# Three openings of a two-block transformer kernel: two output tiles taken slice by slice together, and the low parts moved in VectorE's order

## The chip, the cores and the metric

The kernel runs on one core of one Trainium2 chip. The metric is the device time of one execution in microseconds (us), the median of several runs. The core has five engines that work side by side and meet through semaphores: TensorE (PE, matmuls; PEld is its weight load), VectorE (DVE), ScalarE (ACT), GpSimd (POOL) and SyncE (SP), which here issues most of the DMAs.

## What is computed

The reference runs two transformer blocks on 1024 tokens of width 1024, all in float32. The first block matters here:

```python
h = rmsnorm(x, mix_norm_g)
q, k, v, g, u = split(h @ w_in)                      # 4 heads of retention, 4 pooling groups
y_ret  = silu(g) * head_rmsnorm(retention(rope(q), rope(k), v), ret_gn_g)
y_pool = pool_mixer(u, pool_w, pool_scale)           # means over 2, 4, 8, 16 tokens, then 128x128 products
x = x + concat(y_ret, y_pool) @ w_out                # "the output projection"
x = x + cross_attn(rmsnorm(x, xa_norm_g), mem_n, ...)
x = x + conv_glu_ffn(rmsnorm(x, ffn_norm_g), ...)    # "the feed-forward"
```

The second block (a gated delta rule layer and an attention layer with forget gates) follows and isn't touched.

## The kernel before

Activations lie feature-major: 8 slices (KT = 8) of 128 features by 1024 tokens. Every projection is cut into output tiles of 128 features, and a tile is 48 matmuls of 512 columns: 8 slices, 2 halves of the tokens, and 3 products each (`dot3`, L517 to L519), since each float32 operand is split into a high part (rounded to the matmul's fp32r form) and a low part (the rest), and high by high, high by low and low by high are added. The activation's parts are `h_hi` (made by ACT) and `h_lo` (made by DVE from `h_hi`); a weight tile is loaded by SP into one of two buffers `w_raw`, and POOL makes `w_hi` (L450) and `w_lo` (L452) of it (`split_slot`). Tile t uses weight buffer and PSUM accumulator t % 2. So the weights of tile t+2 can be split only once PE is through with tile t (`pe_slot`), and its matmuls can begin only once tile t was copied out of PSUM (`tile_out`, `tile_added`) and the split is done (`w_split`).

The order on each engine is written out by hand. PE counts the 16 groups of a tile with `s` (`among`) and does the small matmuls of other stages between them.

Launch. SP loads weight tile 0, the 8 slices of x, then weight tile 1, in this order. POOL's queue issues the vectors, the positions and then four sets of constants (L444), before it splits weight tile 0. ACT makes `h_hi` slice by slice (L1249) and then squares x (L1204). DVE computes the rotation angles of the sine (L1823 to L1842), then the 8 low parts (L1846), the sum of the squares (L1777, L1780), the reciprocal root of the first norm (L1851), the angles of the cosine (L1828 to L1840), multiplies both tables, once ACT has taken their sine, by the norm (L1858), and rotates q (L1866 to L1875) and k (L1866 to L1869). PE takes tile 0 slice by slice as the low parts come (`fresh`), then tile 1; the norm's sums (`token_sums`, L591) stand at s = 28, near the end of tile 1, and the norm is spread over the partitions (`spread`, L597) after it. The norm doesn't scale h; it is applied to what comes out of the tiles. Tiles 2 and 3 follow, then the first head's work, which begins with transposes of the rotated k (`turn8`, L617).

Output projection. DVE's last pooling step (`pool(3)`) comes before the low parts of its input (L1960). PE takes tile 20, the first of the projection, over slices 0 to 6, multiplies the last pooling group by its weights (`pool_product(3)`, L662, at s = 13), and waits for slice 7, which comes of that product through ACT and DVE. After the last low part ACT loads the memory tokens `memx` and x again (L1336, L1338), ACT squares and DVE sums `memx`, and DVE adds tile 20 to the loaded x (L1968); tile 22 waits for that addition, tile 23 for that of tile 21.

Feed-forward. After the last addition (L2016) DVE adds the square of the slice before, makes the 8 low parts (L2022) and adds the last square. PE takes tiles 0 and 1 (of the feed-forward), then the norm's sums and its spread; ACT copies the norm out (L1426), DVE copies tile 0 out with it (L2049), and tile 2 waits for that.

## Time and profile before

| | us |
|---|---|
| median of 3 runs (lowest, highest) | 3104.93 (3104.66, 3107.49) |
| the profiled execution | 3107.14 |
| its span, first to last instruction | 3105.3 |
| PE busy in it | 2891.3 (93%) |
| DVE / POOL / ACT busy | 1534.7 / 1057.7 / 802.7 |
| mean granted clock of PE | 0.967 of full |

PE is busy nearly all the time, so what counts is where it stands still or runs at half its clock; the three stages of the change lie at 0 to 90, 319 to 385 and 773 to 820 us of the span.

### The profile page before, as it was taken

The numbers are of one execution on the slowest core, as the hardware profiler recorded it, in microseconds if no ns is written. First come the engines' busy times: TensorE is split into PE (matmuls) and PEld (weight loads), VectorE is DVE, ScalarE is ACT, GpSimd is POOL, SyncE is SP. The second block draws the span as 40 slices with busy tenths as digits, with TensorE's granted clock in tenths as the row PEclk, the third lists the DMA queues.
The fourth block names the chain that finished last, engine by engine and source line by source line (L and its number), as shares of the span: only waits on it lengthen the run. The fifth ranks groups of instructions, "written<-read, shape, count | busy, mean of one in ns | idle before, by whom it ended". The sixth has DMA issues, their size and how long they took to land.

```text
span 3105.3 us, 35553 instructions
## 1 busy us (share of the span) xinstructions
PE 2891.3 (93%) x14278; PEld 2340.3 (75%) x14278; DVE 1534.7 (49%) x1903; ACT 802.7 (26%) x1137; POOL 1057.7 (34%) x473
## 2 busy tenths in 40 slices
PE   7999888989999999999988999999986999999996
PEld 5887677767788888888767888888774777777774
DVE  7334514122666665566845555666537344444434
ACT  4231202231100000000343434444322333333331
POOL 4232366214344444444411212222235333333223
PEclk9999999999999999999989999999997999999997
DMA  3111222001111111111212112222121111011112
GB/s 128 35 35 34 108 75 74 29 14 48 41 48 44 46 47 47 47 47 47 95 56 59 61 52 68 64 64 65 51 90 74 35 35 35 35 40 43 34 35 109
DMA packets 94228, 170.26 MB, mean 55 GB/s; under 512 B 30192, under 2 KB 56976, under 8 KB 93968
## 3 DMA queue, kind: packets, MB, share of 16 engines
q1 hardware_dynamic: 85120, 135.81, 13.4%
q10 hardware_dynamic: 8464, 30.48, 2.5%
q8 instruction: 100, 1.64, 0.2%
q0 software_dynamic: 512, 2.07, 0.2%
q14 instruction: 32, 0.26, 0.0%
HBM read 149.39 MB, written 18.94 MB: 54 GB/s over the span
## 4 chain that ended last, share of the span: by engine, by line
PE 80%; DVE 11%; POOL 3%; issue 3%; ACT 3%; DMA 1%; POOLq 0%; ACTq 0%; DVEq 0%; SPq 0%
PE gemm L517 18%; PE gemm L518 17%; PE gemm L519 17%; PE small L518 3%; PE small L517 3%; PE small L519 3%; PE small L591 3%; PE small L1095 2%; PE small L1117 2%; PE small L967 1%; DVE norm L1780 1%; PE small L1105 1%; POOL xres L495 1%; PE small L617 1%; DVE xres L2530 1%
## 5 line engine op out<-in xcount | busy, mean ns | idle before, releaser
L517 PE MATMUL gemm<-h_hi,w_hi 128*128 128x512 f32 x2688 | 1142.2, 425 | 89.1 <-DVE h_lo L1790 43.4
L518 PE MATMUL gemm<-h_lo,w_hi 128*128 128x512 f32 x2688 | 1074.7, 400 | 0.0
L519 PE MATMUL gemm<-h_hi,w_lo 128*128 128x512 f32 x2688 | 1073.8, 399 | 0.0
L450 POOL TENSOR_TENSOR w_hi<-w_raw,unit_col 128x1024 fp32r<-128x1024 f32 x174 | 341.3, 1962 | 1602.3 <-PE gemm L519 1452.0
L517 PEld LDWEIGHTS gemm<-h_hi,w_hi 128*128 128x128 f32 x2688 | 515.7, 192 | 210.1 <-issue 64.9
L519 PEld LDWEIGHTS gemm<-h_hi,w_lo 128*128 128x128 f32 x2688 | 512.8, 191 | 123.5
L518 PEld LDWEIGHTS gemm<-h_lo,w_hi 128*128 128x128 f32 x2688 | 515.5, 192 | 105.2 <-issue 6.5
L452 POOL TENSOR_TENSOR w_lo<-w_raw,w_hi 128x1024 fp32r<-128x1024 f32 x174 | 466.8, 2683 | 13.7
L486 POOL TENSOR_TENSOR w_hi<-w_raw,unit_col 128x1024 fp32r<-128x1024 f32 x32 | 60.6, 1893 | 374.6 <-PE gemm L519 374.6
L2049 DVE TENSOR_TENSOR norm<-gemm,norm 128x1024 f32<-128x1024 f32 x44 | 53.9, 1226 | 192.1 <-PE gemm L519 189.8
L517 PE MATMUL small<-act_hi,w_hi 128*128 128x512 f32 x352 | 139.3, 396 | 0.0
L518 PE MATMUL small<-act_lo,w_hi 128*128 128x512 f32 x352 | 139.3, 396 | 0.0
L519 PE MATMUL small<-act_hi,w_lo 128*128 128x512 f32 x352 | 139.3, 396 | 0.0
L2080 DVE TENSOR_TENSOR xres<-small,xres 128x1024 f32<-128x1024 f32 x88 | 107.5, 1222 | 58.1 <-PE small L519 58.0
L2058 DVE SCALAR_TENSOR_TENSOR head<-norm,vec,head 128x1024 f32<-128x1024 f32 x44 | 124.6, 2832 | 3.9 <-DVE head L2054 1.2
L1432 ACT ACTIVATE head<-head 128x1024 f32<-128x1024 f32 x22 | 23.3, 1061 | 374.0 <-DVE head L2062 374.0
L2516 DVE SCALAR_TENSOR_TENSOR xres<-small,rstd_cols,xres 128x128 f32<-128x128 f32 x64 | 22.5, 351 | 192.6 <-PE small L1095 172.9
L591 PEld LDWEIGHTS small<-const,norm 128*128 128x128 f32 x688 | 91.9, 211 | 30.7 <-DVE norm L1780 17.3
L591 PE MATMUL small<-const,norm 128*128 128x1 f32 x688 | 89.2, 260 | 25.9 <-DVE norm L1780 18.9
L1662 ACT ACTIVATE xres<-xres,stat 128x128 f32<-128x128 f32 (+3 forms) x64 | 49.7, 777 | 227.0 <-DVE stat L2522 226.1
L1437 ACT ACTIVATE act_hi<-head 128x1024 fp32r<-128x1024 f32 x22 | 23.4, 1062 | 265.5 <-DVE head L2067 265.5
L1117 PEld LDWEIGHTS small<-xres 128*128 128x128 f32 x576 | 74.1, 191 | 8.4 <-ACT xres L1735 2.8
(379 smaller groups left out, 3758.3 us busy)
## 6 DMA issues: line engine op xcount, KB each, us to landing
w_raw<-w_stream SPq DMA_DIRECT2D x206, 512.0 KB, 3.2
x_spill<-xres ACTq DMA_DIRECT2D x16, 512.0 KB, 2.6
xres<-x_spill ACTq DMA_DIRECT2D x16, 512.0 KB, 7.6
xres<-x_t SPq DMA_DIRECT2D x8, 512.0 KB, 13.0
xres<-x_t ACTq DMA_DIRECT2D x8, 512.0 KB, 10.1
xres<-g_rows SPq DMA_DIRECT2D x8, 512.0 KB, 3.8
norm<-g_rows SPq DMA_DIRECT2D x8, 512.0 KB, 3.7
mt_plane<-xres SPq DMA_DIRECT2D x8, 512.0 KB, 3.2
```

What stands on the lines that cost most here:

```text
L450: nc.gpsimd.tensor_tensor(whi[s][:, :, :], raw[s][:, :, :], unit, ALU.mult).then_inc(w_hi_done, 1)
L452: nc.gpsimd.tensor_tensor(wlo[s][:, :, :], raw[s][:, :, :], whi[s][:, :, :].bitcast(F32), ALU.subtract).then_inc(w_split, 1)
L486: nc.gpsimd.tensor_tensor(whi[s][:, :, :], raw[s][:, :, :], unit, ALU.mult).then_inc(w_hi_done, 1)
L517: mm(dst, w_hi, a_hi, start=first, stop=False)
L518: mm(dst, w_hi, a_lo, start=False, stop=False)
L519: return mm(dst, w_lo, a_hi, start=False, stop=last)
L591: last = mm(dst[:, n:n + 1], ck(src, n), ones[:, 0:1], start=True, stop=True)
L1095: last = mm(pa[:, c:c + w], ck(yt[:, g, :], q), H[:, g % 2, c:c + w], start=True, stop=True)
L1117: last = mm(ck(pb, 4 + q % 4), ck(X4(0), b), ck(X4(5), b), start=(b == 0), stop=(b == q))
L2049: V.tensor_tensor(a[:, 2:2 + S], gp[v][:, :], WIDE_FF, ALU.mult).then_inc(tile_out, 1)
L2058: V.scalar_tensor_tensor(c, a[:, 1:1 + S], at("ff_w", 2 * PAIRS + q), c, ALU.mult, ALU.add).then_inc(ff_taps, 1)
L2080: V.tensor_tensor(xres[:, m, :], ps[m % 2][:, :], xres[:, m, :], ALU.add).then_inc(down_ev, 1)
```

## The change

`gemm_pair` takes two tiles together: for each slice first tile t, then tile t+1, so a slice carries 12 matmuls, not 6. Three places use it: tiles 0 and 1 of the launch, tiles 20 and 21 of the output projection, tiles 0 and 1 of the feed-forward. The rest moves with it: the norm's sums and spread of the launch from s = 28 and 31 to 36 and 39 (in tile 2), on PE and on ACT, those of the feed-forward to s = 25 and 28 of the pair's 32 groups, the last pooling product to s = 19 (after slice 4 of the pair). On DVE the low parts and the sums of squares of the launch go ahead of all angles; the low parts 0 to 3 of the output projection go into `pool(3)`, behind its copy out of PSUM and ahead of the pooling itself; one addition of squares in the feed-forward goes from ahead of the low parts to between the last two. On POOL's queue the four loads of constants go between the splits of weight tiles 0 and 1. SP's order stays. ACT waits for the sums of squares before it copies out tile 0 of the launch.

```diff
@@ POOL
-            for dst, src in ((const[:, :], consts), (row[:, :], rows.broadcast_to([P, N_SMALL])),
-                             (small_raw[:, :, :], small_w), (poolw[:, :, :], pool_w)):
-                pool.dma_start(dst, src).then_inc(const_loaded, 16)
...
-            for s in range(2):
-                split_slot(s, s, 1)
+            split_slot(0, 0, 1)
+            for dst, src in ((const[:, :], consts), (row[:, :], rows.broadcast_to([P, N_SMALL])),
+                             (small_raw[:, :, :], small_w), (poolw[:, :, :], pool_w)):
+                pool.dma_start(dst, src).then_inc(const_loaded, 16)
+            split_slot(1, 1, 1)
@@ PE
+            def gemm_pair(t, a_hi, a_lo, fresh, among=None):
+
+                for k in range(KT):
+                    pe.wait_ge(h_lo_done, KT * fresh + k + 1)
+                    for b in range(2):
+                        if k == 0:
+                            pe.wait_ge(w_split, t + b + 1)
+                        for c in range(2):
+                            at = slice(c * HALF, (c + 1) * HALF)
+                            last = dot3(gp[b][:, at], whi[b][:, k, :], wlo[b][:, k, :], a_hi[:, k, at], a_lo[:, k, at],
+                                        k == 0, k == KT - 1)
+                            if k == KT - 1 and c:
+                                last.then_inc(pe_slot, 1)
+                            if among is not None:
+                                among(4 * k + 2 * b + c)
...
-                    if w == 0 and s == 28:
+                    if w == 0 and s == 36:
                         pe.wait_ge(const_loaded, 64)
                         pe.wait_ge(sq_added, KT * (NMIX + 1))
                         token_sums(pa[:, 0:NB], N[:, 2, :]).then_inc(norm_mm, 1)
-                    if w == 0 and s == 31:
+                    if w == 0 and s == 39:
                         pe.wait_ge(norm_rstd, S_MIX + 1)
                         spread(pa, R_H).then_inc(norm_wide, 1)
...
-                for j in range(4):
+                if w == 0:
+                    gemm_pair(T_RET, hhi, hlo, HMIX, among)
+                for j in range(0 if w else 2, 4):
...
-                if s == 2 * (KT - 1) - 1:
+                if s == 19:
                     pool_product(3)
...
+                if i == 0:
+                    gemm_pair(T_WOUT, hhi, hlo, HRET, pool_last)
+                elif i == 1:
+                    continue
...
-            for q in range(4):
-                if q >= 2:
-                    pe.wait_ge(tile_out, EV_FF + q - 1)
-                gemm_tile(T_FF + q, q % 2, hhi, hlo, S, HFF if q == 0 else None)
-                if q == 1:
+            def ff_start(s):
+
+                if s == 25:
                     pe.wait_ge(sq_added, KT * (NFF + 1))
                     token_sums(pa[:, 0:NB], N[:, 2, :]).then_inc(norm_mm, 1)
+                if s == 28:
                     pe.wait_ge(norm_rstd, S_FF + 1)
                     spread(pa, R_H).then_inc(norm_wide, 1)
+
+            gemm_pair(T_FF, hhi, hlo, HFF, ff_start)
+            for q in range(2, 4):
+                pe.wait_ge(tile_out, EV_FF + q - 1)
+                gemm_tile(T_FF + q, q % 2, hhi, hlo, S)
@@ ACT
             act.wait_ge(h_lo_done, KT * (HMIX + 1))
+            act.wait_ge(sq_added, KT * (NMIX + 1))
@@ DVE
+            for k in range(KT):
+                dve.wait_ge(h_hi_done, KT * HMIX + k + 1)
+                V.scalar_tensor_tensor(hlo[:, k, :], xres[:, k, :], vc("mix_g", k), hhi[:, k, :].bitcast(F32), ALU.mult,
+                                       ALU.subtract).then_inc(h_lo_done, 1)
+            for k in range(KT):
+                add_square(NMIX, k)
             dve.wait_ge(pos_loaded, 16)
...
                     done(V.tensor_scalar(dst, dst, -math.pi, None, ALU.max))
-                    for k in range(KT):
-                        dve.wait_ge(h_hi_done, KT * HMIX + k + 1)
-                        V.scalar_tensor_tensor(hlo[:, k, :], xres[:, k, :], vc("mix_g", k), hhi[:, k, :].bitcast(F32), ALU.mult,
-                                               ALU.subtract).then_inc(h_lo_done, 1)
-                    for k in range(KT):
-                        add_square(NMIX, k)
                     dve.wait_ge(norm_root, NMIX + 1)
                     V.reciprocal(R_H, R_H).then_inc(norm_rstd, 1)
...
                 V.tensor_tensor(POOL_U[:, PAD:], gp[t % 2][:, :], WIDE_MIX, ALU.mult).then_inc(tile_out, 1)
+                if j == 3:
+                    for k in range(4):
+                        lo_part(HRET, k, yt[:, k, :], hhi, hlo)
...
-            for k in range(KT):
+            for k in range(4, KT):
                 lo_part(HRET, k, yt[:, k, :], hhi, hlo)
...
-                if m:
+                if 0 < m < KT - 1:
                     add_square(NFF, m - 1)
...
             for k in range(KT):
+                if k == KT - 1:
+                    add_square(NFF, KT - 2)
                 dve.wait_ge(h_hi_done, KT * HFF + k + 1)
```

## Rows read from the trace of the kernel before

**Rows 1.** Page, the chain that ended last, share of the span by engine.

```profile
PE 80%; DVE 11%; POOL 3%; issue 3%; ACT 3%; DMA 1%; POOLq 0%; ACTq 0%; DVEq 0%; SPq 0%
```

**Rows 2.** Waits of PE, 0 to 100 us: who, for whom, us, times, longest.

```profile
PE gemm L517 <- DVE h_lo L1846: 19.7, 1, 19.7
PE small L591 <- DVE norm L1780: 2.9, 1, 2.9
PE small L617 <- DVE head L1869: 2.5, 1, 2.5
```

**Rows 3.** Waits of PE, 280 to 358 us.

```profile
PE gemm L517 <- DVE h_lo L1790: 11.5, 2, 7.9
```

**Rows 4.** Waits of PE, 770 to 812 us.

```profile
PE gemm L517 <- DVE h_lo L2022: 6.5, 1, 6.5
PE gemm L517 <- DVE norm L2049: 2.4, 1, 2.4
```

**Rows 5.** Stretches: us, busy (count) of PE, PEld, DVE, ACT, POOL; clock, DMA, GB/s.

```profile
10.00:15.00 5.00, 0.00 (x0) 0.00 (x0) 4.63 (x6) 2.11 (x2) 0.00 (x0) 1.00 1.01 406
27.10:42.55 15.45, 15.45 (x68) 12.34 (x66) 14.93 (x9) 5.08 (x5) 10.22 (x6) 1.00 0.20 68
49.03:52.95 3.92, 3.92 (x10) 3.01 (x11) 3.34 (x5) 0.27 (x1) 0.00 (x0) 0.51 0.00 0
326.83:339.39 12.56, 12.56 (x43) 10.00 (x43) 6.66 (x6) 0.00 (x0) 0.00 (x0) 0.76 0.00 1
```

**Rows 6.** Timeline of POOL: start, us, instruction, [idle before <-releaser].

```profile
22.22 2.68 POOL L450 TENSOR_TENSOR w_hi<-w_raw,unit_col 128x1024 fp32r<-128x1024 f32 x1 [13.09 <-DMA w_raw<-w_stream]
24.98 3.26 POOL L452 TENSOR_TENSOR w_lo<-w_raw,w_hi 128x1024 fp32r<-128x1024 f32 x1
...
100.50 1.89 POOL L450 TENSOR_TENSOR w_hi<-w_raw,unit_col 128x1024 fp32r<-128x1024 f32 x1 [18.84 <-PE gemm L519]
102.48 2.38 POOL L452 TENSOR_TENSOR w_lo<-w_raw,w_hi 128x1024 fp32r<-128x1024 f32 x1
```

**Rows 7.** Timeline of DVE, launch.

```profile
11.71 0.69 DVE L1828 TENSOR_SCALAR yt<-yt 128x1024 f32<-128x1024 f32 x1
...
18.28 13.56 DVE L1846 SCALAR_TENSOR_TENSOR h_lo<-xres,vec,h_hi 128x1024 fp32r<-128x1024 f32 x8
...
32.95 12.72 DVE L1780 TENSOR_TENSOR norm<-norm 128x1024 f32<-128x1024 f32 x7
49.51 0.20 DVE L1851 RECIPROCAL rstd_cols<-rstd_cols 128x8 f32<-128x8 f32 x1 [3.83 <-ACT rstd_cols L1291]
...
63.22 2.36 DVE L1858 TENSOR_TENSOR yt<-yt,norm 128x1024 f32<-128x1024 f32 x2 [3.32 <-ACT yt L1300]
...
76.57 2.87 DVE L1869 TENSOR_TENSOR head<-head,xres 128x1024 f32<-128x1024 f32 x1
```

**Rows 8.** Timeline of ACT, launch.

```profile
44.01 1.00 ACT L1267 ACTIVATE yt<-gemm 128x1024 f32<-128x1024 f32 x1
```

**Rows 9.** Timeline of DVE, opening of the output projection.

```profile
325.46 8.03 DVE L1790 TENSOR_TENSOR h_lo<-yt,h_hi 128x1024 fp32r<-128x1024 f32 x7
...
354.81 1.22 DVE L1968 TENSOR_TENSOR xres<-gemm,xres 128x1024 f32<-128x1024 f32 x1
```

**Rows 10.** Timeline of ACT, opening of the output projection.

```profile
341.31 1.11 ACT L1282 ACTIVATE yt<-small,vec 128x1024 f32<-128x1024 f32 x1 [15.62 <-PE small L662]
...
349.60 0.73 ACT L1204 ACTIVATE head<-memx 128x256 f32<-128x256 f32 x2 [6.09 <-DMA memx<-mem_t]
```

**Rows 11.** Timeline of DVE, opening of the feed-forward.

```profile
776.17 11.75 DVE L2022 SCALAR_TENSOR_TENSOR h_lo<-xres,vec,h_hi 128x1024 fp32r<-128x1024 f32 x8
...
808.49 1.22 DVE L2049 TENSOR_TENSOR norm<-gemm,norm 128x1024 f32<-128x1024 f32 x1 [2.29 <-ACT norm L1426]
```

**Rows 12.** Timeline of PE, opening of the feed-forward.

```profile
803.81 1.84 PE L591 MATMUL small<-const,norm 128*128 128x1 f32 x16
806.24 1.09 PE L597 MATMUL small<-const,rstd_cols 128*128 128x128 f32 x8 [0.59 <-DVE rstd_cols L2026]
```

More of the change, by code:

```diff
@@ L686, in _ @@
                 among = ret_among(w)
-                for j in range(4):
+                if w == 0:
+                    gemm_pair(T_RET, hhi, hlo, HMIX, among)
+                for j in range(0 if w else 2, 4):
                     t = T_RET + 4 * w + j
-                    if t >= 2:
-                        pe.wait_ge(tile_out, t - 1)
-                    gemm_tile(t, t % 2, hhi, hlo, S, HMIX if t == 0 else None, among, 16 * j)
+                    pe.wait_ge(tile_out, t - 1)
+                    gemm_tile(t, t % 2, hhi, hlo, S, None, among, 16 * j)
             def pool_last(s):
-                if s == 2 * (KT - 1) - 1:
+                if s == 19:
                     pool_product(3)
@@ L709, in _ @@
                         pe.wait_ge(tile_out, EV_MEM + m_out + 1)
-                if kind == "x":
-                    gemm_tile(t, t % 2, hhi, hlo, S, HRET if i == 0 else None, pool_last if i == 0 else None)
+                if i == 0:
+                    gemm_pair(T_WOUT, hhi, hlo, HRET, pool_last)
+                elif i == 1:
+                    continue
+                elif kind == "x":
+                    gemm_tile(t, t % 2, hhi, hlo, S)
                 else:
@@ L1288, in _ @@
                         ret_tile(h, s // 16 - 1)
-                    if w == 0 and s == 28:
+                    if w == 0 and s == 36:
                         act.wait_ge(norm_mm, NMIX + 1)
                         A(R_H, pa[:, 0:NB], ACT.Sqrt, bias=eps[:, 0:1], scale=1.0 / D).then_inc(norm_root, 1)
-                    if w == 0 and s == 31:
+                    if w == 0 and s == 39:
                         act.wait_ge(norm_wide, W_MIX + 1)
```

## The prediction

> **What bounds the kernel now.** I read the page's chain first: PE carries 80% of it and DVE 11% [rows 1], so a change of order gains only where PE stands still, and loses wherever it makes PE stand. Next come PE's own waits in the three stages. At launch there are three: 19.7 us until the first low part, 2.9 us ahead of the norm's sums, 2.5 us ahead of the transposes of the rotated k [rows 2]. At the output projection PE waits twice for a low part, 7.9 and 3.6 us [rows 3]; at the feed-forward 6.5 us for the first low part and 2.4 us for the copy out of tile 0 [rows 4]. Third, PE's pace in stretches [rows 5]: 15.45 us hold 66 matmuls at full clock, 0.234 us each, so a tile of 48 is 11.2 us and a pair's slice of 12 is 2.8; with the clock granted at 0.51 (1.2 GHz of 2.4) nine take 3.92 us, 0.43 each. A matmul at the lower level costs 0.19 us more. Last, the timelines of POOL, DVE and ACT show what ends each wait.
>
> The views also show what no wait shows: the second weight tile is there late. POOL idles 13.09 us for its load, begins its split at 22.22 and ends it at 28.24 [rows 6]. Before the change that costs nothing, since tile 0 alone keeps PE busy from 19.7 on.
>
> **Launch, PE.** The low parts now follow `h_hi` as x arrives; the first is ready near 11 us, not 19.7, and the last near 23.5, not 31.84 (18.28 + 13.56 [rows 7]). But `gemm_pair` needs both weight tiles in slice 0. Six matmuls run, and then PE stands until the second split. SP's order is the same, and the loads run at 406 GB/s with the DMA engines full [rows 5], so the load ends at 22.2 as before; the constants, issued after split 0, still pass in its shadow. Split 2 meets a busy DVE as before (6.0 us [rows 6]); PE resumes at 27.9. Of the remaining 90 matmuls those of about 6 us run at the low level: in the stretch from 326.83, 42 matmuls take 12.56 us, which solves to 6.1 us at 0.427 [rows 5]. I take 14 x 0.427 + 76 x 0.2335 = 23.7, and tile 1 ends at 51.6, tile 0 at 50.2. Before, tile 1 ended at 53.0, with the 2.9 us wait and 9 slow matmuls in it [rows 2, 5]: 1.4 us gained.
>
> It is given back at once. The weights of tile 2 can be split only when tile 0 is through, now 1.4 us ahead of tile 1 and no longer a whole tile ahead. A split without a rival on DVE is 1.89 + 2.38 + 0.1 = 4.35 us [rows 6]; tile 2 starts at 50.2 + 4.4 = 54.6 (before 53.7), after a pause of 3 us. A pause of 2.87 us was followed by matmuls at the low level [rows 2, 5], so I let 4 us of tile 2 run there: 9 matmuls more dear by 0.19, 1.8 us.
>
> **Launch, the norm and the angles.** This is the term that decides. The sums stood at s = 28 and gave the reciprocal at 49.51 to 49.71 [rows 7]. At s = 36 they follow 15 matmuls of tile 2: 54.6 + 15 x 0.2335 + 1.8 = 59.9, plus the sums, 1.84 less overlap, 1.75 [rows 12], and ACT's root and the reciprocal, 0.5: 62.2. ACT is free by then: its six copies of tiles 0 and 1, 1.02 each [rows 8], start at 50.2 and end at 56.4. On DVE the cosine's seven steps stand behind that reciprocal. They took from 49.71 to 59.90 (63.22 less 3.32 idle), with a split beside them; the sine's same seven took 11.71 to 18.28, 6.6 us, without one [rows 7]. After: 62.2 + 6.6 = 68.8, with no split beside them, since tile 3's is over near 59. Three sines on ACT: 3.3, the 3.32 us for which DVE idled [rows 7]. From 72.1 DVE needs two table products and seven rotation steps: before, 63.22 to 79.44, 16.2 us, of which about 5.4 is blocking by splits, seen in one 1.23 us step that took 2.87 [rows 7] and two like it. So 10.8 bare. Tile 2 ends at 54.6 + 11.2 + 1.8 + 1.75 + 0.95 = 70.3 (spread 0.95 from [rows 12]), and its end starts a split that lies on the tables; tile 3 ends at 81.6, and its end starts another. I take 4.4 of blocking: 72.1 + 10.8 + 4.4 = 87.3. Before: 79.5 [rows 7]. PE, whose own path arrives at 82.3, turns k 7.8 us later than now. It then stood 5 us, not 2.5, and I add 0.7 for the clock: **launch +8.5 us**, between +2.8 (PE's own path, 82.3) and +11 (sums and 15 matmuls wholly at the low level).
>
> What PE's earlier start frees is thus hidden behind DVE's angles, which gain a place later in line: the low parts and squares end some 9 us earlier, but DVE then idles from about 45 to 62 for the root.
>
> By the Trainium skill (SBUF — State Buffer, Who interferes with whom), a VectorE instruction with two SBUF inputs and a GpSimd one that reads SBUF block each other wholly, whichever issues second. The trace agrees in kind: L1869 took 2.87 us beside a split [rows 7] and `w_lo` 3.26 beside busy VectorE against 2.38 [rows 6]. Taken to the letter, each step met would lose a whole 2.4 us, the two splits 4.8, and the launch would come to +8.9.
>
> **Output projection.** Low parts 0 to 3 move ahead of the pooling step: four of 1.15 us (8.03 / 7 [rows 9]), behind a copy out at 320.2. With the split of tile 21 on them, the first is ready at 322, not 326.7, and pooling ends at 330.3, not 325.5. PE starts 4.8 us earlier, at the low clock for some 5 us, and does slices 0 to 4 of the pair, 60 matmuls: 322 + 14.0 + 2.2 = 338.2; the product stood at 339.4, after 42 matmuls [rows 5]. It takes 1.9 us; ACT's scaling (1.11 [rows 10]) and high part and DVE's low part follow, 3.5 us, so the last low part is there at 343.6, 1.1 earlier. The pair is done at 348.7, where tile 21 was done at 357.6: nearly 9 us. But tile 22 waits for tile 20's addition to the reloaded x. The reload begins behind the last low part, its first tensor lands 4.8 us later (ACT idles 6.09 for it [rows 10]), then come eight squares and sums, and the addition stood at 354.81 to 356.03 [rows 9]. Less 1.1 and with up to 2 us of blocking by the split of tile 23, which now lies here, tile 22 starts between 354.9 and 357, I take 355.8: 1.8 gained of 8.9. And PE has stood 7 us, so 8 to 14 matmuls at 0.19 extra follow, 1.5 to 2.7 us. **Output projection +0.3**, from -1.5 to +2.
>
> **Feed-forward.** With one addition of squares (1.88 us beside a split) gone from ahead of it, low part 0 is ready at 776.4, where the first stood behind a 776.17 start and came at 779.6 [rows 4, 11]: 3.2 us. The second weight tile is split by 778.5, just in time for slice 0. 96 matmuls 22.4 + about 2.1 for the low clock + sums and spread 2.8 [rows 12], now inside the pair: end at 803.8, tile 0 at 802.4. Its split (4.4 to 5.3) lets tile 2 start at 807.4, where it started at 809.77, 2.4 us after the wait of [rows 4]. The addition of squares between low parts 6 and 7 costs 1.2 us that PE, at 2.8 us a slice, doesn't see. **-2.3 us**, from -4.6 (a clock that stays up) to -1.
>
> By the Trainium skill (TensorE: Matmul & The Clock Gate, HAM oscillation), waits that recur between bursts of matmuls send the gate back to half rate, and the ramp is paid each time. The trace agrees at [rows 5], clock 0.51 after a 2.87 us pause; by that rule all three pairs are followed by such a ramp, which is what the sums have, and each that failed to come would take 1.8 us off.
>
> **Sum.** +8.5 + 0.3 - 2.3 = +6.5 us. Everything after 820 us hangs on PE's chain and moves along. The profiled run took 3107.14 (span 3105.3 + 1.84), 2.2 over the median of 3104.93. Against its own time: 3113.6; for the median: 3104.93 + 6.5 = **3111.4**.
>
> **Rivals.** *The launch delay is half as long.* If the norm's sums come at 59 and the splits miss the rotation, k is ready at 83 to 84 and the launch costs 4; total +1 to +3, 3107. For it: the count of slow matmuls after a pause varies, 9 here and 14 there. Against: the seven cosine steps and the rotation are fixed, 17.4 us.
> *The clock stays up (the other side).* The pairs' pauses are near 3 us, and PE's 2.5 us wait at launch [rows 2] is the shortest known. If PE keeps 2.4 GHz through pauses of 3.2 us, decided at the end of tile 1, the launch costs 2.8 to 4.5, the output projection gains 1.5 to 2 by an earlier product, the feed-forward gains 2.1 in the pair and 1.9 after it, 6.3: total -3.5 to -9, middle 3099 to 3101. Against it stands the 2.87 us pause with its clock of 0.51.
> *It doesn't do what it says.* If the moved constants let the second weight tile come earlier, by at most 1.33 MB / 406 GB/s = 3.3 us (962 + 256 + 96 + 12 KB by their shapes), the launch moves by that: total +3.2, 3108. That needs them to pass after it; they are issued near 9 us, it lands at 22.
>
> **How the numbers follow.** Forecast 0.60, own range 3106 to 3116 (launch +4 to +11 with the other terms' middles, rounded in): slower by over 6.2 us 0.46 of it, the rest within. Half delay 0.18 and earlier weights 0.05, all within 0.2%. Clock stays up 0.17: 0.11 faster, 0.06 within. So slower 0.46, same 0.43, faster 0.11; 0.2% or 6.2 us is about what a measurement of this kernel can tell from none. The range takes in half of the other side's case: 3101 to 3117.
>
> **What would show it.** Launch: six matmuls near 11 us, PE idle until 28, tile 2 near 54.6 behind POOL's `w_lo`, the reciprocal of L1851's twin near 62, PE's wait for the rotated k at 5 us, ending near 87. If it ends at 80, the main term is wrong. Output projection: PE starts at 322, ends the pair near 349 and waits some 7 us for the addition; a wait for `w_lo` in its place would mean that the reload isn't the limit and gain 3 us more. Feed-forward: the wait for the first low part at 3.3 us in place of 6.5, and a wait for `w_lo` of 3.5 in place of 2.4 for the copy (all later positions shifted by the launch's term). The prediction fails if the cosine's steps aren't what PE waits for, or if the clock ignores the pauses.

## The result and the profile after

The changed kernel is slower: 3119.89 us median (3116.96 to 3121.6, 6 runs) against 3104.8 (3101.59 to 3111.26, 6 runs), a ratio of 1.0039 with the 95% interval 1.0029 to 1.0049, that is +12 us (9 to 15). The two medians lie 15.1 us apart; I go by the ratio, which has an interval, here and in all experiments. I had forecast 3111.4, +6.5. The direction was right and the size about half of what came. The median of the runs lies 2.9 us above the upper end of my range (3101 to 3117); the ratio applied to the median I started from gives 3117.0, its very edge.

The profiled run of the changed kernel has the lowest of its six times, 3116.96 us, and that of the kernel before one of the higher (3107.49; the table and the prediction have 3107.14, which no run took), so the two traces, 9.8 us apart in span, show less than the 12. The page of the changed kernel (first its span, then the chain by engine) looks like that of before [rows 1], and PE is busy for 2887.4 us against 2891.3; the sums don't tell the two apart:

```profile
span 3115.1 us, 35554 instructions
...
PE 80%; DVE 10%; POOL 3%; issue 3%; ACT 3%; DMA 2%; SPq 0%; POOLq 0%; ACTq 0%; DVEq 0%
```

PE's waits in the changed kernel, 0 to 100 us (who, for whom, us, times, longest), where [rows 2] stood:

```profile
PE gemm L517 <- POOL w_lo L449: 17.4, 2, 14.1
PE gemm L517 <- DVE h_lo L1849: 10.7, 1, 10.7
PE small L633 <- DVE head L1894: 7.0, 1, 7.0
```

280 to 370 us, where [rows 3] stood:

```profile
PE gemm L517 <- DVE xres L1996: 11.2, 1, 11.2
...
PE gemm L517 <- issue: 3.2, 1, 3.2
```

770 to 830 us, where [rows 4] stood ("issue" is here the first matmul of the pair, which starts as soon as the first low part is there):

```profile
PE gemm L517 <- POOL w_lo L449: 3.6, 1, 3.6
PE gemm L517 <- issue: 3.2, 1, 3.2
```

Launch: the 19.7 us until the first low part became 10.7, but 17.4 us for the weight splits came in, 14.1 in slice 0 for the second tile's and 3.3 behind the pair for the third's; the wait for the rotated k grew from 2.5 to 7.0. Output projection: one wait of 11.2 us for the addition of tile 20, which the kernel before didn't have. Feed-forward: 6.5 became 3.2, and the split, 3.6, took the place of the 2.4 for the copy.

The weights of each tile are split once on POOL. The start of the same split in both traces gives the time by stage:

| Where (split of the tile) | before | after | shift | of the stage |
|---|---|---|---|---|
| tile 20, end of the retention heads | 306.2 | 313.2 | +7.0 | launch +7.0 |
| tile 24, the third split after the pair | 369.1 | 379.5 | +10.4 | output projection +3.4 |
| tile 46 | 523.8 | 537.2 | +13.4 | memory tiles, first query tile +3.0 |
| feed-forward tile 4 | 823.3 | 833.2 | +9.9 | feed-forward -3.5 |
| end of span | 3105.3 | 3115.1 | +9.8 | rest -0.1 |

**Launch.** POOL's timeline (start, us, instruction, idle before): the load of the second weight tile ends at 22.0 and its split at 27.7, as before [rows 6]; the split for tile 2 can start only at 49.70, where before it started at 34.0, and PE takes tile 2 up at 54.2.

```profile
22.02 2.90 POOL L447 TENSOR_TENSOR w_hi<-w_raw,unit_col 128x1024 fp32r<-128x1024 f32 x1 [10.94 <-DMA w_raw<-w_stream]
24.99 2.67 POOL L449 TENSOR_TENSOR w_lo<-w_raw,w_hi 128x1024 fp32r<-128x1024 f32 x1
...
49.70 1.90 POOL L447 TENSOR_TENSOR w_hi<-w_raw,unit_col 128x1024 fp32r<-128x1024 f32 x1 [17.84 <-PE gemm L519]
51.67 2.34 POOL L449 TENSOR_TENSOR w_lo<-w_raw,w_hi 128x1024 fp32r<-128x1024 f32 x1
```

DVE: the reciprocal of the root, the table products after ScalarE's sines, the last step of the rotation of k, which came at 49.51, 63.22 and 76.57 [rows 7]:

```profile
59.92 0.20 DVE L1876 RECIPROCAL rstd_cols<-rstd_cols 128x8 f32<-128x8 f32 x1 [14.89 <-ACT rstd_cols L1316]
...
69.97 4.75 DVE L1883 TENSOR_TENSOR yt<-yt,norm 128x1024 f32<-128x1024 f32 x2 [3.32 <-ACT yt L1325]
...
85.81 1.23 DVE L1894 TENSOR_TENSOR head<-head,xres 128x1024 f32<-128x1024 f32 x1
```

ACT in the same stretch, the wide copy of the norm and the first sine:

```profile
62.68 1.03 ACT L1319 ACTIVATE norm<-small 128x1024 f32<-128x1024 f32 x1 [2.80 <-PE small L613]
...
66.68 1.06 ACT L1323 ACTIVATE yt<-yt 64x1024 f32<-64x1024 f32 x1 [1.67 <-DVE yt L1871]
```

The reciprocal is 10.4 us late, k 7.6. PE turns k at 87.18, where it was 79.58; its own path had arrived at 80.1.

**Output projection.** POOL's splits of tiles 22 and 23, then DVE from the first sum of the memory tokens to the two additions to x, where [rows 9] has the addition at 354.81:

```profile
353.68 1.90 POOL L447 TENSOR_TENSOR w_hi<-w_raw,unit_col 128x1024 fp32r<-128x1024 f32 x1 [22.48 <-PE gemm L519]
355.65 2.34 POOL L449 TENSOR_TENSOR w_lo<-w_raw,w_hi 128x1024 fp32r<-128x1024 f32 x1
357.95 2.08 POOL L447 TENSOR_TENSOR w_hi<-w_raw,unit_col 128x1024 fp32r<-128x1024 f32 x1
360.11 2.40 POOL L449 TENSOR_TENSOR w_lo<-w_raw,w_hi 128x1024 fp32r<-128x1024 f32 x1
```

```profile
355.39 0.34 DVE L1802 COPY head<-head 128x256 f32<-128x256 f32 x1 [5.37 <-ACT head L1228]
355.83 9.07 DVE L1805 TENSOR_TENSOR head<-head 128x256 f32<-128x256 f32 x7
364.82 2.35 DVE L1996 TENSOR_TENSOR xres<-gemm,xres 128x1024 f32<-128x1024 f32 x2
```

Seven sums took 9.07 us. In the kernel before the same seven took 3.60 (351.29 to 354.89). An unhindered one takes 0.42; of the seven here three took 2.45, 1.93 and 2.38, each beside one of POOL's last three instructions.

**Clock.** Stretches of the changed kernel (us; busy and count of PE, PEld, DVE, ACT, POOL; granted clock; DMA share and GB/s): the 15 matmuls of tile 2 of the launch that stand ahead of the norm's sums, tile 22, and the first query tile, then that query tile in the kernel before.

```profile
54.16:57.74 3.58, 3.58 (x16) 2.89 (x16) 0.00 (x0) 2.95 (x3) 3.50 (x2) 1.00 0.44 146
366.09:379.13 13.04, 13.04 (x48) 10.45 (x49) 1.08 (x1) 0.00 (x0) 0.00 (x0) 0.85 0.07 29
521.16:534.52 13.36, 13.36 (x48) 10.65 (x48) 7.12 (x3) 0.00 (x0) 5.96 (x2) 0.78 0.24 78
```

```profile
510.43:521.16 10.73, 10.73 (x48) 8.71 (x48) 7.16 (x3) 0.00 (x0) 6.00 (x2) 1.00 0.28 98
```

Tile 2 of the launch ran at full clock behind a pause of 3.2 us. Tile 22 follows a pause of 11.2 us and has a clock of 0.85, nine slow matmuls. The query tile's code isn't part of the change: 13.36 us in one trace at a clock of 0.78 and 10.73 in the other at 1.00, 2.6 us.

### The profile page after: what moved, and what is told of

The parts are those of the page before. It is cut to its first block, busy times and chain, and to the rows that moved or that the text cites. A ratio compares the mean times of both kernels' runs of the same rounds, so it can differ in the third digit from the quotient of the medians.

```text
span 3115.1 us, 35554 instructions
## 1 busy us (share of the span) xinstructions
PE 2887.4 (93%) x14278; PEld 2333.4 (75%) x14278; DVE 1537.7 (49%) x1903; ACT 803.2 (26%) x1137; POOL 1059.0 (34%) x473
## 4 chain that ended last, share of the span: by engine, by line
PE 80%; DVE 10%; POOL 3%; issue 3%; ACT 3%; DMA 2%; SPq 0%; POOLq 0%; ACTq 0%; DVEq 0%
PE gemm L517 18%; PE gemm L518 17%; PE gemm L519 17%; PE small L517 3%; PE small L518 3%; PE small L519 3%; PE small L607 3%; PE small L1119 2%; PE small L1141 2%; PE small L991 1%; PE small L1129 1%; POOL xres L495 1%; PE small L633 1%; DVE xres L2560 1%; DVE norm L1805 1%
```

## The experiments

Two theories stood at the start. A: the three parts of the change add up, the launch loses by the late norm, the output projection by blocked sums, the feed-forward gains. B: one of them is harmless, or its gain or loss is the clock's. Ratios below are to the kernel before, with 95% intervals; 0.001 is 3.1 us.

**1. The launch's part alone**, the kernel before with the POOL, ACT and DVE steps of the launch and tiles 0 and 1 as a pair.

```diff
-            for s in range(2):
-                split_slot(s, s, 1)
+            split_slot(0, 0, 1)
...
+            split_slot(1, 1, 1)
...
-                    if w == 0 and s == 28:
+                    if w == 0 and s == 36:
...
+                if w == 0:
+                    gemm_pair(T_RET, hhi, hlo, HMIX, among)
```

> The launch's part of the change alone (constants after split 0, tiles 0 and 1 as a pair, low parts and squares ahead of the angles, the norm's sums at s = 36). Theory A, the three parts add up: the wait for the rotated k ends near 87 us where it ended at 79.6 before, and every later stage is 7.0 us late; +7 us in the profile, ratio near 1.0023. Rival B, the launch is harmless and the loss of some 12 us comes from the other two parts: k ready by 80 us, ratio within 1.000 +- 0.001.

Measured: 1.0049 (1.0032 to 1.0066), 3121.63 us. A's direction stands; its size, 1.0023, lies below the interval. The trace shows why. The stretch that ran at full clock in the changed kernel (3.58 us for 15 matmuls) is here:

```profile
54.71:61.02 6.31, 6.31 (x16) 4.95 (x17) 0.00 (x0) 2.95 (x3) 4.08 (x2) 0.52 0.42 127
```

6.31 us at half clock, for the same code behind the same pause of 3.24 us. DVE's reciprocal and the last step of k:

```profile
63.19 0.20 DVE L1869 RECIPROCAL rstd_cols<-rstd_cols 128x8 f32<-128x8 f32 x1 [18.31 <-ACT rstd_cols L1309]
...
89.08 1.22 DVE L1887 TENSOR_TENSOR head<-head,xres 128x1024 f32<-128x1024 f32 x1
```

The reciprocal moves with it, to 63.19, and k is ready at 90.3: the launch costs 11.3 us in this trace (split of tile 20 at 317.5) and 7.0 in that of the changed kernel. In both, k comes 26.9 us after the reciprocal's end. Run 7, whose launch is that of the changed kernel, has the clock at 0.53 there too and costs 11.4. I had written 4 us of half clock into tile 2; what came was none, some (5.1 us for the 15 matmuls, in run 4), or all.

**2. The output projection's part alone.**

```diff
+                if i == 0:
+                    gemm_pair(T_WOUT, hhi, hlo, HRET, pool_last)
...
+                if j == 3:
+                    for k in range(4):
+                        lo_part(HRET, k, yt[:, k, :], hhi, hlo)
...
-            for k in range(KT):
+            for k in range(4, KT):
```

> The output projection's part alone (tiles 20 and 21 as a pair, low parts 0 to 3 inside the last pooling step, product at s = 19). Theory A, the split of tile 23's weights now lies on VectorE's eight sums of the memory tokens and blocks them: tile 20's addition ends 10 us after the reload's first tensor lands instead of 5, tile 22 starts 1.5 us later than in the kernel before (357.6), 8 to 14 slow matmuls follow: +3 to +4 us, ratio 1.0011. Rival B, as my forecast had it, the addition waits for the reload and its few sums alone: tile 22 starts 1 to 2 us earlier, total within +-1 us.

Measured: 1.0008 (0.9997 to 1.0019). PE's wait in its trace, 280 to 372 us:

```profile
PE gemm L517 <- DVE xres L1991: 11.2, 1, 11.2
```

Tile 22 starts at 359.0 and not at 357.6, nine slow matmuls follow, and the third split after the pair is 3.5 us late: A, and not my forecast. The interval alone, +2.5 us (-1 to +6), wouldn't have told.

**3. The feed-forward's part alone.**

```diff
+            gemm_pair(T_FF, hhi, hlo, HFF, ff_start)
+            for q in range(2, 4):
...
-                if m:
+                if 0 < m < KT - 1:
...
+                if k == KT - 1:
+                    add_square(NFF, KT - 2)
```

> The feed-forward's part alone (its tiles 0 and 1 as a pair, the norm's sums and spread inside it, one addition of squares moved). Theory A: the wait for the first low part falls from 6.5 to 3.2 us, a wait of 3.6 us for the split of tile 2 takes the place of 2.4 + 0.6 us: 3 us gained, ratio 0.9990. Rival B, the gain seen in the changed kernel was the clock's phase: 0 to 1 us.

Measured: 0.9988 (0.9979 to 0.9998), 3.7 us gained; in the trace 3.4 between the splits of the feed-forward's tiles 0 and 4. PE's waits, 750 to 830 us:

```profile
PE gemm L517 <- POOL w_lo L452: 3.6, 1, 3.6
PE gemm L517 <- issue: 3.2, 1, 3.2
```

A. The three parts measured alone give +15.2, +2.5 and -3.7, in sum +14, where the whole gave +12 (9 to 15): they add up within intervals of 3 to 5 us each.

**4. The root behind the cosine's angles.** The change by itself:

```diff
                     done(V.tensor_scalar(dst, dst, -math.pi, None, ALU.max))
-                    dve.wait_ge(norm_root, NMIX + 1)
-                    V.reciprocal(R_H, R_H).then_inc(norm_rstd, 1)
                     settle()
+            dve.wait_ge(norm_root, NMIX + 1)
+            V.reciprocal(R_H, R_H).then_inc(norm_rstd, 1)
```

> The changed kernel with one move: the wait for the norm's root and its reciprocal go behind both angle tables, so VectorE does the cosine's steps while it would idle from 45 to 60 us. Theory A, the launch's loss is the cosine's seven steps standing behind a root that now comes 10 us later: ScalarE takes the sines as soon as its copies are done, k is ready before TensorE asks for it at 80.1, and the launch is 7 us shorter than in the changed kernel: 7 us off, level with before plus 3. Rival B, the loss lies in the rotation that the splits block: at most 2 us off.

Measured: 1.0045 (1.0028 to 1.0062), against 1.0039 of the changed kernel: nothing gained. My theory A fell here. B had the time right (at most 2 us off) but isn't the loss: blocking in the table products and the rotation was 6.3 us in the changed kernel and 5.4 before, 0.9 of the 7.6 by which k is late. ACT:

```profile
61.78 0.27 ACT L1316 ACTIVATE rstd_cols<-small,eps 128x8 f32<-128x8 f32 x1 [5.18 <-PE small L607]
64.85 1.03 ACT L1319 ACTIVATE norm<-small 128x1024 f32<-128x1024 f32 x1 [2.80 <-PE small L613]
65.90 1.28 ACT L1323 ACT_TABLE_LOAD   x1
67.19 1.06 ACT L1323 ACTIVATE yt<-yt 64x1024 f32<-64x1024 f32 x1
```

The cosine's steps were done at 55.2, 11 us earlier than in the changed kernel, but ACT does root, wide copy, table load and only then the sines, in its written order. The sine starts 4.9 us after the reciprocal (62.28) and not 6.6 (66.68 after 60.12). This gain of 1.7 us was lost: tile 2 began 0.6 us later, its first 15 matmuls took 1.5 us more, and after the sines the splits cost 1.2 us more of blocking (70.48 to 88.79). So two chains run beside each other behind the sums, DVE's cosine and ACT's wide copy, and I had seen only the first. New theory C: the place of the sums itself holds everything.

**5. The norm's sums early in the pair.** On the changed kernel:

```diff
-                    if w == 0 and s == 36:
+                    if w == 0 and s == 20:
                         pe.wait_ge(const_loaded, 64)
...
-                    if w == 0 and s == 39:
+                    if w == 0 and s == 24:
                         pe.wait_ge(norm_rstd, S_MIX + 1)
...
-                    if w == 0 and s == 36:
+                    if w == 0 and s == 14:
                         act.wait_ge(norm_mm, NMIX + 1)
...
-                    if w == 0 and s == 39:
+                    if w == 0 and s == 15:
                         act.wait_ge(norm_wide, W_MIX + 1)
```

> The changed kernel with the launch's norm moved into the pair: sums at s = 20 and spread at s = 24 on TensorE (36 and 39 in the change), and on ScalarE the root and the wide copy ahead of the copies of tiles 0 and 1; nothing else moves. Moving the root behind the cosine's steps gained nothing: the sines on ScalarE began at 67 us all the same, behind the root and the wide copy that stand ahead of them in its order. Theory C, the late place of the norm's sums holds everything (ScalarE's order, then the tables): sums near 43 us, sines from 57 to 60.5, k ready near 75, before TensorE is through with tile 3 (79 to 82, the sums' 2.8 us now lie in the pair); the 7 us wait for k goes, the launch ends 6 us earlier than in the changed kernel. Rival D, the rotation blocked by the splits would hold k past 84 even so: at most 3 us off.

Measured: 1.0008 (0.9999 to 1.0017), 3108.95 us, 9.6 us under the changed kernel by the ratios. DVE:

```profile
47.19 0.20 DVE L1876 RECIPROCAL rstd_cols<-rstd_cols 128x8 f32<-128x8 f32 x1 [1.19 <-ACT rstd_cols L1316]
...
63.60 2.36 DVE L1883 TENSOR_TENSOR yt<-yt,norm 128x1024 f32<-128x1024 f32 x2 [8.11 <-ACT yt L1325]
...
76.96 1.23 DVE L1894 TENSOR_TENSOR head<-head,xres 128x1024 f32<-128x1024 f32 x1
```

PE's transposes of k follow tile 3 without a pause:

```profile
81.00 1.04 PE L633 MATMUL small<-const,head 128*128 128x128 f32 x8
```

k is ready at 78.2 and not near 75, as ACT's sines came at 60.3 and not at 57, behind its copies; that is still 2.8 us before PE asks. The loss of the launch is gone: k is turned at 81.0 (79.6 before), and the split of tile 20 starts at 305.97, where it started at 306.17 before. C stands: it was the norm moved to s = 36 that cost, and not the pair.

**6. The second weight tile loaded earlier.**

```diff
-            for t in range(2):
-                sp.dma_start(raw[t][:, :, :], w_stream[t]).then_inc(w_loaded[t], 16)
-                if t == 0:
-                    for k in range(KT):
-                        sp.dma_start(xres[:, k, :], x_t[k]).then_inc(x_loaded[k], 16)
+            sp.dma_start(raw[0][:, :, :], w_stream[0]).then_inc(w_loaded[0], 16)
+            for k in range(KT):
+                sp.dma_start(xres[:, k, :], x_t[k]).then_inc(x_loaded[k], 16)
+                if k == 1:
+                    sp.dma_start(raw[1][:, :, :], w_stream[1]).then_inc(w_loaded[1], 16)
```

> The changed kernel with SyncE's load of weight tile 1 moved from behind all of x to behind x's slice 1. Theory A (TensorE stands 14 us in slice 0 for that weight tile alone): the split of tile 1 is done near 16 us, the pair ends near 31 instead of 51, tile 2 follows at 35 and the norm's sums wait for the squares, near 38 us; then the angles on VectorE are last: k near 73 instead of 87, launch 12 to 15 us shorter than in the changed kernel, 4 to 7 shorter than before. Rival E, the loads share the same full queue, so what weight tile 1 gains x loses and the low parts come as late: pair ends past 45 and less than 4 us is won.

Measured: 1.0014 (1.0005 to 1.0023), 7.8 us under the changed kernel by the ratios; 8.0 in the trace. POOL:

```profile
13.68 3.20 POOL L449 TENSOR_TENSOR w_lo<-w_raw,w_hi 128x1024 fp32r<-128x1024 f32 x1
...
38.52 2.96 POOL L447 TENSOR_TENSOR w_hi<-w_raw,unit_col 128x1024 fp32r<-128x1024 f32 x1 [15.15 <-PE gemm L519]
```

The split is done at 16.9, as A said, but the pair ends at 39.7, between A's 31 and E's 45. PE doesn't stop once between 16.93 and 39.7: the 90 matmuls that are left take 21 us at 0.2335 each, and eight or nine slow ones the rest. A's 31 was a wrong sum, and x came in time, so E is out. PE's waits:

```profile
PE gemm L517 <- POOL w_lo L449: 8.5, 2, 5.2
PE small L633 <- DVE head L1894: 7.0, 1, 7.0
```

The wait for k is again 7.0 us: the reciprocal ends at 52.2, k is ready 26.9 us later, at 79.1. The pair ended 11.2 us earlier, the root came 7.9 earlier and so did k, where A had 14: here an earlier start of the pair is worth what it moves the root. The launch is 1.0 us shorter than in the kernel before (split of tile 20 at 305.17), where A had 4 to 7.

**7. The additions to x ahead of the memory tokens' sums.**

```diff
-            for k in range(KT):
-                add_square(NMEM, k)
             def add_x(i, m):
...
             for m in range(2):
                 add_x(m, m)
+            for k in range(KT):
+                add_square(NMEM, k)
```

> The changed kernel with VectorE's additions of tiles 20 and 21 to x moved ahead of the eight sums of the memory tokens' squares. Theory A, the additions are late because three of the eight small sums before them are blocked by the weight splits (2 us and more each, where one takes 0.42): the addition of tile 20 follows the landing of x's slice 0 at once, tile 22 starts near 358.5 instead of 366.1, 7 us off, some of it given back where the memory norm comes later. Rival F, the reload itself is what holds tile 22: it starts no more than 1 us earlier.

Measured: 1.0007 (0.9998 to 1.0016), 9.9 us under the changed kernel by the ratios. In the trace 9.7 between the splits of tiles 20 and 24. DVE:

```profile
360.88 2.50 DVE L1993 TENSOR_TENSOR xres<-gemm,xres 128x1024 f32<-128x1024 f32 x2 [6.42 <-DMA xres<-x_t]
363.29 1.15 DVE L1802 COPY head<-head 128x256 f32<-128x256 f32 x1
364.54 5.67 DVE L1805 TENSOR_TENSOR head<-head 128x256 f32<-128x256 f32 x7
```

PE's wait at tile 22:

```profile
PE gemm L517 <- POOL w_lo L449: 3.2, 1, 3.2
```

The addition starts at 360.88, as x's first slice lands, and PE waits 3.2 us, for the split of tile 22's weights and for nothing else, where it waited 11.2; and no slow matmuls follow (clock 1.00 from 362.5 to 366.5). Tile 22 starts at 362.58, 3.5 us earlier, in a trace whose launch is 4.4 us longer: 7.9 us by the start and 1.8 by the clock. The seven sums still lose 2.1 us to a split (5.67 against 3.60), behind the additions, where no wait of PE shows. A stands; the sums held the addition back, and the reload's landing is what it waits for now.

**8. Both mends together**, the norm early and the additions first.

The edits are those of 5 and 7, side by side.

> The norm early in the pair (as in the run before with the sums at s = 20) and the additions of tiles 20 and 21 ahead of the memory tokens' sums, on the changed kernel. If the two losses are apart, as the single runs say (the wait for k gone: launch level with before; the addition no longer blocked: output projection 6 us shorter than before; feed-forward 3 us shorter): 9 us under the kernel before, ratio 0.997. If the clock's phase eats them, as the medians of the single runs hint (1.0008 and 1.0007), ratio 0.999 to 1.000.

Measured: 0.9979 (0.997 to 0.9988), 6.5 us (4 to 9) under the kernel before; the 0.997 of two separate losses is the edge of the interval, the 0.999 of the rival lies outside. In the trace the launch is level with before (split of tile 20 at 306.18), the output projection 5.0 us shorter, the feed-forward 3.4. The two losses are apart. The last step of k in it, blocked by a split, still comes in time for PE at 82.4:

```profile
73.92 3.30 DVE L1894 TENSOR_TENSOR head<-head,xres 128x1024 f32<-128x1024 f32 x1
```

**9. Weight tile 1 early, sums at s = 28, additions first.** As in 6 and 7, with the sums on PE from s = 36 to 28 and the root on ACT from s = 36 to 14.

```diff
-                    if w == 0 and s == 36:
+                    if w == 0 and s == 28:
                         pe.wait_ge(const_loaded, 64)
...
-                    if w == 0 and s == 36:
+                    if w == 0 and s == 14:
                         act.wait_ge(norm_mm, NMIX + 1)
```

> Weight tile 1 loaded after x's slice 1, the norm's sums at s = 28 of the pair (root on ScalarE ahead of the copies of tiles 0 and 1; spread stays at s = 39), the additions of tiles 20 and 21 first. In four profiles k was ready 27.1 us (31 where the sines wait for the copies) after the reciprocal of the root. Theory C: with the pair ending near 40 and the root near 38, the reciprocal follows the sine's angles at 47 to 48, k is ready at 74 to 75 and launch is 5 us shorter than before; with 6 and 3 from the other two, 14 us under the kernel before, ratio 0.9955. Rival: the reciprocal isn't what k follows, and k stays at 79: ratio 0.997.

Measured: 0.9976 (0.9967 to 0.9986), no more than run 8 within the intervals. ACT's root, its wide copy and the first sine:

```profile
41.46 0.27 ACT L1316 ACTIVATE rstd_cols<-small,eps 128x8 f32<-128x8 f32 x1
...
54.45 1.03 ACT L1319 ACTIVATE norm<-small 128x1024 f32<-128x1024 f32 x1 [6.65 <-PE small L613]
...
56.80 1.06 ACT L1323 ACTIVATE yt<-yt 64x1024 f32<-64x1024 f32 x1
```

DVE's last step of the cosine's angles:

```profile
55.69 0.69 DVE L1871 TENSOR_SCALAR yt<-yt 128x1024 f32<-128x1024 f32 x1
```

The root came at 41.5, 18 us before that of the changed kernel, but k was ready at 78.4, 34.2 us after the reciprocal. The rival was right in the time of k. Two chains end together ahead of the sine at 56.8. The spread had stayed at s = 39, in tile 2 behind the pause, so the wide copy came at 54.45 and the table load behind it. And the cosine's seven steps now lie beside the splits of tiles 2 and 3 and take 12.3 us (44.06 to 56.38), where they take 6.6 alone. An earlier spread would have brought the sine 0.4 us at most. The launch is 1.8 us shorter than before (split of tile 20 at 304.33), not 5.

**10. The pairs' last three slices tile by tile**, on the kernel of run 9, at the launch and the feed-forward.

```diff
+                order = [(k, b) for k in range(KT - tail) for b in range(2)] + \
+                    [(k, b) for b in range(2) for k in range(KT - tail, KT)]
-                for k in range(KT):
+                for n, (k, b) in enumerate(order):
```

> The kernel of the run before it, with the last three slices of the pairs at the launch and the feed-forward taken tile by tile (tile 0's, then tile 1's), so that tile 0 is through 4.2 us ahead of tile 1 and not 1.4. Theory S, the 3 to 5 us pause behind each pair is the split of the third tile's weights, which starts only when tile 0 is through: the pause falls by 2.8 us in both places, 3 us less at the feed-forward and up to 3 at the launch if k doesn't hold it: 3 to 6 us under the run before it. Rival: the pause is the copy out of tile 0 and the pauses stay.

Measured: 0.9969 (0.9957 to 0.9981), 3096.18 us. Against run 9 that is 2.2 us by the ratios and 5.4 by the medians, with intervals that overlap; the whole program doesn't confirm the 3 to 6 us, the trace does (6.4 at the split of the feed-forward's tile 4). PE's waits, 0 to 100 us and then 750 to 830:

```profile
PE small L634 <- DVE head L1895: 7.2, 1, 7.2
PE gemm L517 <- POOL w_lo L449: 2.7, 1, 2.7
PE gemm L517 <- ACT xres L1295: 2.5, 1, 2.5
```

```profile
PE gemm L517 <- DVE norm L2079: 0.4, 1, 0.4
```

At the feed-forward the 3.6 us for the split are gone, 0.4 us for a copy stands in their place, and with the pause went the eight slow matmuls behind it: the stage is 8.2 us shorter than before, where run 9's was 3.4. S stands there. At the launch the pause fell from 4.1 to 2.5 us and what ends it is now ACT's copy, so there the rival has a part: once the split is early, the copy is next. k is still what PE waits for, 7.2 us; the wide copy and the table load are done at 54.6 here and the sine waits until 56.69 for the cosine's last step. Those steps begin only at 50.0, since the sine's seven ahead of them took 13.9 us beside the splits of tiles 2 and 3, and not 6.6. This version has the lowest ratio, 9.6 us (6 to 13) under the kernel before.

## Why the prediction was right in direction and short in size

**The second weight tile** (right). Six matmuls at 10.7 (forecast 11), PE idle until 27.7 (27.9), pair done at 50.9 (51.6). The constants passed in the load's shadow. The rival of earlier weights fell in the trace of the change itself: the tile landed at 22.0.

**The split behind the pair** (right). Pause 3.2 us, tile 2 at 54.16 (54.6), and a pause of the same kind at the feed-forward, 3.6. Run 10 showed it there by taking it away.

**The launch's term** (right in place, wrong in one reason, and near in size partly by luck). Forecast +8.5 with k at 87.3; the trace has +7.0 and k at 87.0. The late norm was the cause (run 5). The cosine's seven steps did end last ahead of the sine, but only by 1.7 us; run 4 took them away and gained nothing, since ACT's wide copy and table load stand behind the root too (the sine came 4.9 us after the reciprocal all the same). I had not seen that chain. The agreement of k hides two misses: the reciprocal ended 2.1 us earlier than I said, since tile 2 kept full clock, and the blocking after the sines, 4.4 us in my sum, was 6.3 by its rows (69.97 to 87.04, 10.8 bare). PE's own path arrived at 80.1 and not at 82.3, so its wait was 7.0 us and not 5.

**The clock** (a step too sure, and the second term that was too small). I gave tile 2 four slow us as if it were a price. Of the three traces with the change's launch one has no slow matmul among those 15, and two (runs 1 and 7) have about 14; run 4, with the same order on PE, has 8. With 14 the launch costs 11.3 and 11.4, 2.8 more than I forecast. The launch's part alone measured +15 (10 to 20), so the profiled run of the changed kernel, whose tile 2 kept full clock, lies at the low end, as its time does among the six. My own range stopped at a launch of +11. The rival "the clock stays up" fell in its price: in the profiled run the clock did stay up behind the launch's pause, and the launch cost 7.0, not 2.8 to 4.5. Its total was summed wrong as well: by its own terms it is -3.3 to -5.5, not -3.5 to -9.

**The output projection** (the term that failed): forecast +0.3, measured +3.4 in the trace. The step was "with up to 2 us of blocking by the split of tile 23". Two splits, those of tiles 22 and 23, now follow each other without a pause (353.7 to 362.5) and lie on the sums from 355.8 on; the seven sums took 9.07 us and not 3.60, 5.5 us of blocking, in three steps of 1.5 to 2.0 us. I had the cause and took the price of one blocked step, where three were blocked one after the other, each by one of POOL's instructions. Tile 22 started 1.5 us later than before, relative to its stage, not 1.8 earlier, behind a pause of 11.2 us and not 7. Run 7 showed it: with the additions ahead of the sums the stage is 9.7 us shorter than in the changed kernel. The product itself came when I said, the last low part 1.7 us earlier relative to its stage (forecast 1.1).

**The feed-forward** (right): forecast -2.3, trace -3.5, alone -3.7 (-0.6 to -6.5).

**The stages after** (a step left out). I let everything else move along. The memory tiles and the first query tile took 3.0 us more, in untouched code, 2.6 of them in one tile by its clock. Relative to the kernel before, the same stretch stood at between -0.6 and +3.0 in the other traces: +3 in runs 4 and 6, in the same query tile, and -0.3 in run 5, whose code is equal from the output projection on. So it comes and goes with equal code. Whether the change makes it more frequent isn't shown: the traces of runs 1 and 3, with the output projection of before, have 0.0 and -0.6. My range had no term for it.

Two mechanisms that the prediction weighed came out so. Blocking between VectorE and GpSimd decided the output projection: a sum that takes 0.42 us alone took 1.9 to 2.5 beside a split. That is how the Trainium skill (SBUF — State Buffer, Who interferes with whom) has it for two inputs in SBUF, and the trace agrees. Half clock behind a pause came at tile 22, 11.2 us of pause, and only sometimes behind 3.2. The Trainium skill (TensorE: Matmul & The Clock Gate, HAM oscillation) has the engine start at half rate behind waits that recur between its bursts of matmuls. The traces agree at 11.2 us (clock 0.85 over tile 22, 9 slow matmuls) and go both ways at 3.2.

What stays open: how much of the gap between the traces (+9.8) and the ratio (+12) is the clock of tile 2, since only one run of each kernel is profiled. A launch of +11.3 with the other two stages as traced gives +11.2. But a single trace scatters by more than that gap where nothing was changed: behind the feed-forward's tile 4 runs 1, 2 and 3 differ from the kernel before by -3.5, +3.3 and -3.1 us.

## What to carry to other kernels

Where two tiles are taken together to cover a slow operand, look first for what else must be there in their first slice, and for what the third tile needs of the first: the pair at the launch waited 14 us for its second weights and 3 us for the split behind it; at the feed-forward a tail taken tile by tile took the wait for the split away, 3.6 us down to 0.4. When a small reduction moves later so as not to wait, follow all chains that start from it, on every engine in its written order: here three stood close behind each other, the cosine's steps, the wide copy with its table load, and the blocked rotation, and taking one away alone gained nothing. And when an engine's work is drawn together in time, price the blocking by the number of steps in the stretch, and put first the step that the bottleneck waits for.

## What the runs showed of the hardware that I had not expected

After pauses of the same length, 3.24 us, the next 15 matmuls ran at a granted clock of 1.00 in the changed kernel's trace and 0.52 in run 1's, 3.58 against 6.31 us, with equal code ahead. Length alone doesn't order them either: in the kernel before, an idle of 2.4 us ahead of the feed-forward's tile 2, behind the norm's small matmuls, was followed by a clock of 0.51 (809.77 to 814.10). And two VectorE additions of 128x1024 with one input in PSUM took 2.50 us together in run 7, though splits ran on GpSimd from 360.09 to 364.28, all along them; beside splits of the same kind, in the changed kernel, SBUF sums a quarter of their size were stretched from 0.42 to 1.9 to 2.5 us.
